# Odd layer of a hybrid diffusion block: the product of a block's second output put behind the next convolution, loads ahead of its store, the fourth root ahead of X1's first copy

## What is computed

```python
def _rglru_coeffs(xs, w_ra, b_ra, w_ri, b_ri, lam):
    ...
    r = jax.nn.sigmoid(blockdiag(w_ra, b_ra))
    i = jax.nn.sigmoid(blockdiag(w_ri, b_ri))
    log_a = LRU_C * r * jax.nn.log_sigmoid(lam)
    a = jnp.exp(log_a)
    b = jnp.sqrt(-jnp.expm1(2.0 * log_a)) * i * xs
    return a, b

def _odd_mixer(u_lat, u_ctx, ...):
    z = u_lat @ w_in
    zc = u_ctx @ w_in[:, :W_RNN]
    x_l = _dwconv(z[..., :W_RNN], conv_w, left) + conv_b
    x_c = _dwconv(zc[..., :W_RNN], conv_w, left) + conv_b
    ...
    h_ctx_T, y_c = _bidir_scan(a_c, b_c, 0)     # over the context, both directions
    _, y_l = _bidir_scan(a_l, b_l, h_ctx_T)     # h = a * h + b; the directions are added
    y_lat = (y_l * jax.nn.silu(z[..., W_RNN:])) @ w_out
```

## Time and profile before

| | us |
|---|---|
| runs | 2447.99, 2441.50, 2447.63 |
| their median | 2447.63 |
| the profiled execution, its own time | 2441.66 |
| its span, first to last instruction | 2439.8 |
| PE busy in it | 2270.2 (93%) |
| VectorE, ScalarE, GpSimd busy | 1501.9, 1189.5, 514.2 |

### The profile page before, as it was taken

The page is one execution under the profiler, slowest core; times in us unless marked ns, Lnnn a source line. Parts: engine busy times, 40 slices in busy tenths (PEclk is TensorE's granted clock), DMA queues, the critical chain, the costliest instruction groups (busy, mean ns, idle before and its releaser), DMA issues. The chain is left out here.

```text
span 2439.8 us, 34401 instructions
## 1 busy us (share of the span) xinstructions
PE 2270.2 (93%) x12000; PEld 1975.0 (81%) x12000; DVE 1501.9 (62%) x2368; ACT 1189.5 (49%) x1714; POOL 514.2 (21%) x303
## 2 busy tenths in 40 slices
PE   4799999999999999999997999799999999995998
PEld 3688888888888888888875888688898889884887
DVE  5176575765757657576586346566775685576534
ACT  4244434445344453434444234276686577667422
POOL 1423232332313223132221100112111211210300
PEclk7899999999999999999998999899999999997999
DMA  6211111211121111111107555101111111113744
GB/s 244 61 50 60 55 55 52 73 49 55 56 74 51 49 63 56 65 51 49 54 26 267 155 160 164 41 27 69 52 43 43 52 69 43 43 52 125 227 152 142
DMA packets 165346, 199.70 MB, mean 82 GB/s; under 512 B 51064, under 2 KB 125944, under 8 KB 162168
## 3 DMA queue, kind: packets, MB, share of 16 engines
q1 hardware_dynamic: 155304, 174.53, 22.1%
q10 hardware_dynamic: 9792, 23.07, 2.7%
q0 software_dynamic: 144, 0.52, 0.1%
HBM read 166.11 MB, written 31.98 MB: 81 GB/s over the span
## 5 line engine op out<-in xcount | busy, mean ns | idle before, releaser
L950 PE MATMUL ps<-u_hi,w_hi 128*128 128x512 f32 (+1 forms) x1536 | 559.4, 364 | 16.6 <-POOL w_lo L637 16.6
L950 PE MATMUL ps<-u_hi,w_lo 128*128 128x512 f32 (+1 forms) x1536 | 544.8, 355 | 0.0
L950 PE MATMUL ps<-u_lo,w_hi 128*128 128x512 f32 (+1 forms) x1536 | 543.9, 354 | 0.0
L950 PEld LDWEIGHTS ps<-u_hi,w_hi 128*128 128x128 f32 x1536 | 290.4, 189 | 53.6 <-POOL w_lo L637 16.7
L950 PEld LDWEIGHTS ps<-u_hi,w_lo 128*128 128x128 f32 x1536 | 290.2, 189 | 41.9
L950 PEld LDWEIGHTS ps<-u_lo,w_hi 128*128 128x128 f32 x1536 | 291.0, 189 | 37.2
L1524 POOL TENSOR_TENSOR o_w_lo<-o_w_raw,o_w_hi 128x1024 fp32r<-128x1024 f32 x48 | 124.7, 2599 | 715.4 <-ACT o_w_hi L1539 715.4
L1784 PE MATMUL ps<-u_hi,o_w_hi 128*128 128x426 f32 (+2 forms) x640 | 238.3, 372 | 14.0 <-POOL o_w_lo L1524 9.3
L742 ACT ACTIVATE probs<-probs,neg_max 128x640 f32<-128x640 f32 (+1 forms) x160 | 122.8, 768 | 251.8 <-DVE neg_max L858 250.7
L637 POOL TENSOR_TENSOR w_lo<-w_stage,w_hi 128x1024 fp32r<-128x1024 f32 x64 | 153.3, 2395 | 425.5 <-ACT w_hi L695 425.5
L1784 PE MATMUL ps<-u_hi,o_w_lo 128*128 128x426 f32 (+2 forms) x640 | 237.5, 371 | 0.0
(11 more groups left out here) (176 smaller groups left out, 4287.8 us busy)
## 6 DMA issues: line engine op xcount, KB each, us to landing
y_tile<-y_scratch SPq DMA_DIRECT2D x72, 512.0 KB, 5.0
w_stage<-in_w_even SPq DMA_DIRECT2D x64, 512.0 KB, 3.3
o_w_raw<-in_w_odd SPq DMA_DIRECT2D x48, 512.0 KB, 3.3
ada_piece<-in_w_ada SPq DMA_DIRECT2D x16, 1024.0 KB, 5.2
wout_raw<-in_w_out SPq DMA_DIRECT2D x16, 1024.0 KB, 9.9
ada_pieces<-in_w_ada SPq DMA_DIRECT2D x4, 2048.0 KB, 18.3
y_scratch<-h_backward SPq DMA_DIRECT2D x16, 512.0 KB, 2.7
h_scratch<-h_tile ACTq DMA_DIRECT2D x18, 256.0 KB, 2.3
```

The costliest lines, as they stand in the source:

```text
L950: last = nc.tensor.matmul(ps[:, bank(j, g), 0:t - f], w[:, slot, c * P:(c + 1) * P], x[:, c, f:t], start=(c == 0 and n == 0), stop=(c == K ...
```

## The change

VectorE no longer makes the block's second output in one go. `combine` is split in two, `add_streams` (the add) and `gate_streams` (the product). At the end of body n the order is now: recur(n, 3), x_lo of the next block's first half, the convolution of the next block's second half, the add, x_lo of that half, the product. The convolution and that x_lo thereby leave the start of the next body; block 0's are in the prologue. The x_lo that stood inside `recur(n, 3)` stands behind it.

On ScalarE the root of the fourth pass stands ahead of x_hi and of X1's first copy, and the high part of GW0 is made at the end of the body, behind these, and no longer behind X1's third copy.

On SyncE the loads of the next block's Z1 and GW1 stand ahead of the store of the second output. `y_done` starts at 1, so that the tanh of Z0 may run while the previous block's second product is outstanding; that of Z1 may not.

```diff
                 if not last:
-                    load(n + 1, Z0)
-                    load(n + 1, GW0)
+                    for j in (Z0, GW0, Z1, GW1):
+                        load(n + 1, j)
                 store(n, 1)
...
-                act.wait_ge(y_done, 2 * n)
+                act.wait_ge(y_done, 2 * n + mm)
...
                 evacuate(0, X1, 0)
+                split_hi(0, GW0)
 
             def body(n, last):
                 for g in range(1, NG):
                     evacuate(n, X1, g)
-                split_hi(n, GW0)
                 tanh_z(n, Z0, 0)
...
                 if not last:
                     split_hi(n + 1, Z0)
+                root(n, 3)
+                if not last:
+                    evacuate(n + 1, X1, 0)
                     x_hi(n, 0)
-                    evacuate(n + 1, X1, 0)
-                root(n, 3)
+                    split_hi(n + 1, GW0)
...
-            def combine(n, s, link):
+            def add_streams(n, s, link):
                 dve.wait_ge(scan_done, n * 4 + (3 + s))
                 link(nc.vector.tensor_tensor(H1[:, s, 0:LAT], H1[:, s, 0:LAT], H0[:, s, 0:LAT], ALU.add))
+
+            def gate_streams(s):
...
             def body(n, last):
...
-                conv(n, 1, 2 * n + 1, link)
                 silu_z(n, Z0, 0)
-                x_low(n, 1)
                 silu_z(n, Z0, 1)
...
-                combine(n, 0, link)
+                add_streams(n, 0, link)
+                gate_streams(0)
                 if not last:
                     conv(n, 0, 2 * n + 2, link)
-                recur(n, 3, link, None if last else lambda: x_low(n, 0))
-                combine(n, 1, link)
+                recur(n, 3, link)
+                if not last:
+                    x_low(n, 0)
+                    conv(n + 1, 1, 2 * n + 3, link)
+                add_streams(n, 1, link)
+                if not last:
+                    x_low(n + 1, 1)
+                gate_streams(1)
```

More of the change, by code:

```diff
@@ L1474, in prologue @@
                     sp.dma_start(dst if name in ("b_ra", "b_ri") else dst[:], a[name]).then_inc(s_const, 16)
-                for j in range(3):
+                for j in range(5):
                     load(0, j)
@@ L1497, in store @@
             def store(n, mm):
-                sp.wait_ge(y_done, 2 * n + (mm + 1))
+                sp.wait_ge(y_done, 2 * n + (mm + 2))
                 sp.dma_start(dram["y1"][2 * n + mm], H1[:, mm, 0:LAT]).then_inc(y_stored[mm], 16)
             def body(n, last):
-                for j in (Z1, GW1) if last else (Z1, GW1, X0):
-                    load(n, j)
                 if not last:
+                    load(n, X0)
                     load(n + 1, X1)
@@ L1688, in silu_z, with recur @@
                                                op1=ALU.mult).then_inc(bank_free[bank(j, g)], 1)
-            def recur(n, p, link, between=None):
+            def recur(n, p, link):
                 s = p % 2
@@ L1698, in recur @@
                                                op0=ALU.add, op1=ALU.mult).then_inc(v_done, 1)
-                if between:
-                    between()
                 dve.wait_ge(root_done, n * 4 + (p + 1))
@@ L1747, in prologue @@
                 dve.wait_ge(consts_done, 1)
+                dve.sem_inc(y_done, 1)
                 conv(-1, 0, 0, first)
                 x_low(-1, 0)
+                conv(0, 1, 1, first)
+                x_low(0, 1)
             def body(n, last):
```

## The result

| | kernel before | changed kernel |
|---|---|---|
| runs, us | 2441.50, 2447.18, 2447.63, 2447.99 | 2413.99, 2414.87, 2415.12, 2415.82 |
| median, us | 2447.40 | 2414.99 |
| the profiled execution, own time / span | 2441.66 / 2439.8 | 2415.12 / 2413.3 |

The ratio of the runs is 0.9873 with a 95% interval of 0.9857 to 0.9888: 1.3% faster. The forecast was 2416 us, from a sum of 2413.0 for the profiled execution.

A forecast was written before the change was run, and what follows sets the result against it. PE was taken as the bound, losing time in the odd layer's x_lo waits and slow clock behind them. Waits 17.3 plus clock 11.4 give 28.7 us off 2441.66: 2413.0, plus half the 6.0 us run spread: 2416 us, range 2406 to 2430.

The forecast's parts named there:

- What bounds: Odd layer: PE, 93% busy, loses 25.0 us in 8 gate waits for x_lo, plus an estimated 11.4 us of slow clock.
- VectorE's path, 2.4 us a block: Block boundary: the second half's convolution starts 2.4 us earlier, cutting PE's wait from 3.50 to 1.1 us.
- Waits, 17.3 us: PE's gate waits for x_lo: 14.4 us saved in blocks 1 to 6, 1.8 in block 7, 1.1 in block 0.
- ScalarE costs nothing: Root moved ahead of X1's first copy: the copy still ends 0.2 us before PE's third X1 group wants the bank.
- SyncE costs nothing: Loads ahead of the second output's store: only a scan 60 us later needs that store, which waits some 2 us.
- Clock, 11.4 us, all returned: Slow clock behind the gate waits: none after waits of 1.1 us, as in block 0; bounds 0 and 11.4.
- The sum, 28.7 us: Waits 17.3 plus clock 11.4 us, off the profiled execution's 2441.66, giving 2413.0 us.
- The six microseconds between the profiled execution and the median: Runs of the kernel before: spread may be clock falls in these waits or lie elsewhere; half taken, giving 2416 us.
- (A): Rival: GpSimd's split and VectorE overlap or it slips into a free place, 7.7 us more gained, 2408 us; chance 0.07.
- (B): Rival: waits shrink but clock still falls, or ScalarE adds small waits; 2419 to 2424, up to 2430 us; chance 0.22.
- (C): Rival: something ahead of the moved convolution holds VectorE, wait stays 3.5 us; within 7 us of 2447; chance 0.04.
- (D): Rival: late GW0 weights delay X1's second copy and Z0's projection; 2483 us if landing takes 20 us; chance 0.02.

The follow-up runs named there:

- output_ahead: Changed kernel with the second output's add and product back ahead of x_lo and the second convolution; ScalarE and SyncE keep the change: 2442.38 us, ratio 0.9988.
- xlo_silu: Changed kernel, first half's x_lo behind the second convolution, add behind both x_lo, Z1's second silu step inside pass 1 ahead of its root wait: 2402.35 us, ratio 0.9824.
- root_late: Changed kernel with ScalarE's root of the fourth pass back behind x_hi and X1's first copy: 2429.96 us, ratio 0.9934.
- gw0_late: Changed kernel with ScalarE's high part of GW0 back behind X1's third copy: 2414.71 us, ratio 0.9875.
- store_first: Changed kernel with SyncE's store of the second output back ahead of the loads of Z1 and GW1: 2433.59 us, ratio 0.9961.
- vector_alone: Kernel before with only VectorE's order changed and what it needs elsewhere; root, loads and GW0's high part in the old order: 2444.67 us, ratio 1.0013.
- no_gw0_split: Changed kernel, GpSimd makes only 16 of 1024 columns of GW0's low part; gates of passes 0 and 1 use the high part instead: 2405.77 us, ratio 0.9834.
- gw0_split_twice: Changed kernel with GpSimd's work on GW0 doubled, the high part subtracted a second time in place: 2432.21 us, ratio 0.9947.
- add_ahead: Changed kernel with the add alone back ahead of x_lo and the second convolution, the product left at the end: 2429.81 us, ratio 0.9935.

## Why the prediction was right, point by point

- **What bounds.** The waits for x_lo and the slow clock behind them, as far as this change reaches: output_ahead brings both back by putting 2.4 us onto VectorE's path. They weren't PE's only waits in the layer: the seven for silu_gate, 3.7 us, are in the kernel before too, and xlo_silu wins 3 us by them.
- **VectorE's path, 2.4 us a block.** Measured 2.53: the wait fell from 3.50 to 0.97, not to 1.1. The root's product ended 1.34 us after the split (1818.79 to 1820.13; the text said 1.36), the split of GW0 2.20 us after the scan (2.24), x_lo 1.36 after that. Convolution to PE's start is 9.21 us in both kernels (1835.94 - 1826.73). The add was hidden with 0.29 us to spare.
- **Waits, 17.3 us.** Measured 18.5 (25.0 - 6.5): 0.13 us more in each of blocks 1 to 6, and block 7, given 1.1 us, had 0.71.
- **ScalarE costs nothing.** Right: the copy ended at 1818.87, 0.4 us ahead of the third group at 1819.27, where 0.2 was forecast, because it began as the root ended. What the prediction didn't say is that the root's place is a condition of the gain and worth 15 us of it (root_late). It priced only the risk of the move.
- **SyncE costs nothing.** Right for the order as changed, and again only half told: the old order would have cost 18.6 us. The prediction looked at whether something waits for the store, and not at what stood behind the store in the old order.
- **Clock, 11.4 us, all returned.** Measured 9.9 between block 1's and block 7's gates, where the sum had 10.0, and 1.1 behind block 7's, where it had 1.3. The wait of block 0 was a single row, but the right one to go by: the granted clock is 1.00 through blocks 0 to 6 of the changed kernel and of gw0_late, and in store_first it fell only behind the longer waits for o_w_lo. The length of the wait is not the whole mechanism, though (last section).
- **From sum to forecast.** The sum, 28.7 us, was 29.1 in the odd layer. That the forecast came within 1.0 us of the median is in part luck. The six microseconds between the profiled execution and the median were split in halves, 3 us added, and the changed kernel has no such gap (2415.12 and 2414.99); what filled the 3 us in its profiled execution was the even layer, 2.6 us longer, which the prediction didn't have. The six were probably clock for the greater part, which is argued and not shown: the changed kernel's runs lie within 1.8 us, those before within 6.5, and of output_ahead, which has the waits back, within 9.4; of the 13 executions of the kernel before run beside it the fastest (2439.28) had a mean granted clock of 0.973, those above 2448 had 0.967 to 0.969. Against it, vector_alone spreads over 13.7 us and had 0.973 at 2450.81.
- **Rivals.** (A), that the exclusion doesn't bite, is out by no_gw0_split and gw0_split_twice. The reason given against it, that both splits lengthened a VectorE instruction by their own length, read the rows too generously: x_lo took 3.07 us for 1.50 and the product 3.30 for 1.23, so 1.6 and 2.1 us longer, for splits of 2.8 and 2.5. Its price was 7.7 us; without the split the medians are 9.2 us apart. (B) didn't happen with waits of 1 us and does, about every second time, with 2.3. (C) and (D) didn't happen; a late load of GW0 wasn't tried, but that of Z1 in store_first took the path that (D) describes.

## What to carry to other kernels

Work that nobody waits for belongs behind the work that the busiest engine waits for, also when the two are one operation to their author, as an add and a product are here. But a result made later is a semaphore raised later: look at what is queued behind each waiter in its queue, here two weight loads behind a store, or the gain comes back as a wait elsewhere, as all of it did with VectorE's change alone. And a wait of the matrix engine of some microseconds can cost half as much again in slow clock (11 us beside 25.0 us of waits in the kernel before), so cutting it to one microsecond can be worth more than its length.

## What the runs showed of the hardware

GpSimd and VectorE exclude each other for whole instructions, and two kinds that the trace before hadn't shown are held as well: a copy of 20 columns with one input took 2.38 us (0.17 in the kernel before), a tap with one tensor input 3.02 for 0.94. A scan took 2.76 for 0.69; scans were held in the kernel before too, of 1024 columns for up to 4.30 us where they take 2.35. It goes both ways: GpSimd's subtraction of 16 columns, in no_gw0_split, took 2.20 us because it began in a scan:

```profile
1739.48 2.20 POOL L1531 TENSOR_TENSOR o_w_lo<-o_w_raw,o_w_hi 128x16 fp32r<-128x16 f32 x1 [2.28 <-ACT o_w_hi L1544]
```

The Trainium skill's SBUF — State Buffer (Who interferes with whom) says that `copy` and `tensor_scalar` can enter modes that contend with GpSimd, when their operands meet its conditions; the two rows agree. The held copy kept ScalarE idle for 2.8 us ahead of its gate reads; PE, six groups ahead, didn't notice.

The length of a wait alone doesn't tell whether the clock falls. In the profiled executions it fell behind six of the seven waits of 2.9 to 3.5 us of the kernel before and all seven of output_ahead (3.1 to 3.4 us); behind waits of 2.0 to 2.3 us for x_lo four times in seven in add_ahead and in root_late and five in seven in vector_alone; behind store_first's waits of 2.1 to 2.6 us for o_w_lo only two times in seven. And behind the waits of 2.8 to 3.0 us of gw0_split_twice it fell in none of seven; the stretch has 1.00 throughout:

```profile
1590.00:2180.00 590.00, 565.34 (x2768) 518.85 (x2767) 421.91 (x279) 423.22 (x489) 157.91 (x50) 1.00 0.14 51
```

Its other runs reach from 2426.5 to 2434.3 us, and the three slowest had a mean granted clock of 0.971 to 0.973 where the profiled one had 0.975, so there it probably fell; no profile of them shows where. The Trainium skill's TensorE: Matmul & The Clock Gate (What's actually happening) has the chip look at activity on a beat of its own that doesn't start with the kernel, which would fit the alternation of add_ahead and the none of gw0_split_twice; that it is the cause was not tested and stays open.
